# Where the decay masks of the later layers live, and in which order heads and norm blocks are worked off

## What is computed

```python
def step(state, inp):
    xc, lac, bc, cc = inp
    acs = jnp.cumsum(lac, axis=1)
    seg = acs[:, :, None] - acs[:, None, :]
    lmat = jnp.where(mask, jnp.exp(jnp.where(mask, seg, 0.0)), 0.0)
    cb = jnp.einsum('bign,bjgn->bijg', cc, bc)
    y = jnp.einsum('bijgr,bjgrp->bigrp', cb[..., None] * lmat, xc)
    ...
ys = ssd_scan(xs * dtp[..., None], dtp * a, bm, cm)
ys = ys + d_skip * xs
ys = ys.reshape(bsz, s, SSD_INNER) * jax.nn.silu(z)
ysg = ys.reshape(bsz, s, SSD_GROUPS, SSD_INNER // SSD_GROUPS)
ysg = ysg * lax.rsqrt(jnp.mean(ysg * ysg, axis=-1, keepdims=True) + EPS)
ys = ysg.reshape(bsz, s, SSD_INNER) * ssd_norm_w
o_ssd = ys @ ssd_out
```

## Time and profile before

| what | value |
| --- | --- |
| median of 3 runs | 2138.44 us (2137.98 to 2140.2) |
| the profiled execution: its own time | 2139.59 us |
| its span in the profile | 2137.8 us |
| share of the span busy: PE, DVE, ACT, POOL | 99%, 77%, 56%, 3% |
| granted TensorE clock, mean | 0.997 |
| memory traffic over the span | 179 GB/s |

### The profile page before, as it was taken

The page is one execution under the profiler, slowest core; times in us unless marked ns, Lnnn a source line. Parts: engine busy times, 40 slices in busy tenths (PEclk is TensorE's granted clock), DMA queues, the critical chain, the costliest instruction groups (busy, mean ns, idle before and its releaser), DMA issues.

```text
span 2137.8 us, 47790 instructions
## 1 busy us (share of the span) xinstructions
PE 2113.5 (99%) x18652; PEld 2055.5 (96%) x18652; DVE 1640.1 (77%) x2620; ACT 1195.2 (56%) x1803; POOL 58.5 (3%) x54
## 2 busy tenths in 40 slices
PE   9999999999999999999999999999999999999998
PEld 8999999999999999899999999999899999999998
DVE  8987877987877776778957877776678947877764
ACT  6646644565555445546648745445446658845443
POOL 0000000000000000000002200000000002200000
PEclk9999999999999999999999999999999999999999
DMA  7434655654446556554455566556554556565553
GB/s 251 159 128 141 204 190 186 195 171 142 151 157 215 190 189 206 187 168 158 161 190 191 167 203 208 186 187 213 185 169 148 169 183 193 174 201 186 187 189 127
DMA packets 109984, 385.00 MB, mean 180 GB/s; under 512 B 12480, under 2 KB 16768, under 8 KB 109312
## 3 DMA queue, kind: packets, MB, share of 16 engines
q1 hardware_dynamic: 101664, 368.66, 52.2%
q10 hardware_dynamic: 8160, 14.04, 2.1%
HBM read 381.53 MB, written 1.11 MB: 179 GB/s over the span
## 4 chain that ended last, share of the span: by engine, by line
PE 89%; DVE 6%; ACT 2%; issue 2%; DMA 0%; DVEq 0%; ACTq 0%
PE acc L777 25%; PE acc L779 24%; PE acc L778 24%; DVE w_lo L1811 2%; PE acc L896 1%; PE acc L897 1%; PE acc L898 1%; PE acc L841 1%; PE acc L843 1%; PE acc L842 1%; ACT w_hi L1310 1%; PE mid L1133 1%; PE mid L1214 1%; DVE pr L2564 0%; PE mid L964 0%
## 5 line engine op out<-in xcount | busy, mean ns | idle before, releaser
L1811 DVE TENSOR_TENSOR w_lo<-w_raw,w_hi 128x1024 fp32r<-128x1024 f32 x694 | 848.5, 1227 | 306.8 <-ACT w_hi L1310 297.9
L1310 ACT CAST w_hi<-w_raw 128x1024 fp32r<-128x1024 f32 x694 | 724.7, 1047 | 541.3 <-PE acc L779 473.5
L777 PE MATMUL acc<-h_hi,w_hi 128*128 128x256 f32 x2096 | 599.4, 286 | 0.3 <-DVE w_lo L1811 0.3
L779 PE MATMUL acc<-h_hi,w_lo 128*128 128x256 f32 x2096 | 587.5, 280 | 0.0
L778 PE MATMUL acc<-h_lo,w_hi 128*128 128x256 f32 x2096 | 586.3, 280 | 0.0
L777 PE MATMUL acc<-g_hi,w_hi 128*128 128x256 f32 x1456 | 410.0, 282 | 0.8 <-DVE w_lo L1811 0.7
L779 PE MATMUL acc<-g_hi,w_lo 128*128 128x256 f32 x1456 | 407.2, 280 | 0.0
L778 PE MATMUL acc<-g_lo,w_hi 128*128 128x256 f32 x1456 | 406.8, 279 | 0.0
L777 PEld LDWEIGHTS acc<-h_hi,w_hi 128*128 128x128 f32 x2096 | 395.7, 189 | 7.7 <-issue 5.7
L779 PEld LDWEIGHTS acc<-h_hi,w_lo 128*128 128x128 f32 x2096 | 396.1, 189 | 0.0
L778 PEld LDWEIGHTS acc<-h_lo,w_hi 128*128 128x128 f32 x2096 | 395.1, 188 | 0.5
(11 more groups left out here) (434 smaller groups left out, 3394.3 us busy)
## 6 DMA issues: line engine op xcount, KB each, us to landing
w_raw<-weights_d SPq DMA_DIRECT2D x695, 512.0 KB, 3.9
even<-rows_d ACTq DMA_DIRECT2D x16, 256.0 KB, 4.3
odd<-rows_d ACTq DMA_DIRECT2D x32, 128.0 KB, 3.4
p<-p_d ACTq DMA_DIRECT2D x3, 1080.0 KB, 8.5
rdec<-decay_d ACTq DMA_DIRECT2D x2, 768.0 KB, 5.3
p<-p_d SPq DMA_DIRECT2D x1, 1024.0 KB, 10.7
out_d<-work SPq DMA_DIRECT2D x4, 256.0 KB, 2.3
x_all<-x_d SPq DMA_DIRECT2D x1, 516.0 KB, 4.3
```

Source lines behind the costliest of these rows:

```text
L777: mm(dst, wh, hi[:, k, :], start=first and j == 0, stop=False)
L779: done = mm(dst, wl, hi[:, k, :], start=False, stop=last and j == len(ks) - 1)
L1310: nc.scalar.copy(w_hi[:, slot, :], w_raw[:, slot, :]).then_inc(hi_done, 1)
L1811: tt(w_lo[:, slot, :], w_raw[:, slot, :], w_hi[:, slot, :].bitcast(F32), SUB).then_inc(lo_v, 1)
```

## The change

- The product `lseg * cb` is written over the mask itself. `mt`'s space becomes a third mask buffer: `masks` has three, pair b uses `masks[b % 3]`. `pair` on DVE no longer waits for TensorE; `seg` on ACT waits from b = 3 on for `pair_y` b-3 (before: from b = 2 on for `pair` b-2).
- In `ORDER2`, `pair_y` tasks stand two by two (0 and 1 at position 14, 2 and 3 at 18, and so on to 14 and 15 at 37; before, 16 single ones from 17 to 40). The first three `seg` stand at positions 5, 9 and 13 (before: 13, 13, 20), the `cb` tasks at 3, 5, 7, 9 (before: 3, 6, 9, 12).
- The mean's bank is `mid[1]`, and `pair_y` no longer waits for `v_zm`.
- `z_ln` and `z_nt` run three times, over groups (0), (1, 2) and (3), the middle one on two groups at once (`Z_ROOTS`).
- `z_norm`, `z_cast`, `z_low` of blocks 4 to 15 stand at positions 38 to 45, two blocks in each (before: 41 to 47, up to four in one). `z_m` 3 stands at 41 (before: 43).

```diff
 ORDER2 = {
     1: (("rows",),),
     3: (("cb", 0),),
...
-    40: (("pair_y", 15), ("ys", 15), ("z_sq", 12), ("z_mul", 15)),
-    41: (("z_norm", 4), ("z_low", 3), ("z_cast", 4), ("z_norm", 5), ("z_low", 4), ("z_norm", 6), ("z_sq", 13),
...
+    39: (("z_mul", 15), ("z_low", 4), ("z_norm", 6), ("z_cast", 6), ("z_low", 5), ("z_norm", 7), ("z_cast", 7),),
+    40: (("z_low", 6), ("z_norm", 8), ("z_cast", 8), ("z_low", 7), ("z_norm", 9), ("z_cast", 9),),
...
+Z_ROOTS = (0, 1), (1, 3), (3, 4)
...
-        mt = in_arena("mt", 94208, [P, 2, TRI])
+        lseg3 = in_arena("lseg3", 94208, [P, 2, TRI])
+        masks = (lseg[:, 0, :, :], lseg[:, 1, :, :], lseg3[:, :, :])
...
-                if b % 2 and means_ahead(b):
-                    pe.wait_ge(v_zm, at.n * 4 + means_ahead(b))
-                dst = mid[2 + b % 2]
+                dst, mask = mid[2 + b % 2], masks[b % 3]
...
                 pe.wait_ge(p_zsum, at.n * 4 + (g + 1))
-                pe.wait_ge(v_ys, at.n * 16 + values_ahead(g))
-                mm(mid[3][:, 0:T], con1("ones_i"), zq[:, :], start=True, stop=True).then_inc(pe_zm, 1)
+                if g:
+                    pe.wait_ge(v_zm, at.n * 4 + g)
+                mm(mid[1][:, 0:T], con1("ones_i"), zq[:, :], start=True, stop=True).then_inc(pe_zm, 1)
...
-                if b >= 2:
-                    act.wait_ge(v_m, at.n * 16 + (b - 1))
+                if b >= 3:
+                    act.wait_ge(pe_y2, at.n * 16 + (b - 2))
...
-                if b:
-                    dve.wait_ge(pe_y2, at.n * 16 + b)
-                else:
+                if b == 0:
                     dve.wait_ge(v_cb, at.n * 4 + 4)
                 both = cbm[:, b // 4, :].unsqueeze(1).to_broadcast([P, 2, TRI])
-                tt(mt[:, :, :], lseg[:, b % 2, :, :], both, MUL).then_inc(v_m, 1)
+                tt(masks[b % 3], masks[b % 3], both, MUL).then_inc(v_m, 1)
```

More of the change, by code:

```diff
@@ L220 @@
     3: (("cb", 0),),
[L221 to L248, removed]
@@ L257 @@
[L257 to L262, removed]
@@ L263 @@
-    46: (("z_cast", 13), ("z_low", 13), ("z_norm", 15)),
-    47: (("z_cast", 14), ("z_low", 14), ("z_cast", 15), ("z_low", 15)),
+    5: (("cb", 1), ("seg", 0),),
+    7: (("cb", 2),),
+    9: (("cb", 3), ("seg", 1),),
+    13: (("pair", 0), ("pair", 1), ("seg", 2),),
+    14: (("pair_y", 0), ("pair_y", 1),),
+    15: (("ys", 0), ("ys", 1), ("pair", 2), ("seg", 3),),
+    16: (("z_mul", 0), ("z_mul", 1),),
+    17: (("pair", 3), ("seg", 4),),
+    18: (("pair_y", 2), ("pair_y", 3),),
+    19: (("ys", 2), ("ys", 3), ("seg", 5), ("pair", 4),),
@@ new lines @@
+    20: (("z_mul", 2), ("seg", 6), ("pair", 5),),
+    21: (("pair_y", 4), ("pair_y", 5), ("z_mul", 3),),
+    22: (("ys", 4), ("ys", 5), ("seg", 7), ("pair", 6),),
+    23: (("z_mul", 4), ("seg", 8), ("z_mul", 5),),
+    24: (("pair", 7), ("z_m", 0), ("z_ms", 0),),
+    25: (("pair_y", 6), ("pair_y", 7), ("z_ln", 0), ("pair", 8), ("z_nt", 0),),
+    26: (("ys", 6), ("ys", 7), ("seg", 9),),
+    27: (("z_mul", 6), ("pair", 9), ("seg", 10), ("z_mul", 7),),
+    28: (("pair_y", 8), ("pair_y", 9), ("pair", 10),),
@@ new lines @@
+    29: (("ys", 8), ("ys", 9), ("seg", 11),),
+    30: (("z_mul", 8), ("pair", 11), ("seg", 12), ("z_m", 1), ("z_ms", 1), ("z_mul", 9), ("z_norm", 0),
+         ("z_cast", 0), ("z_norm", 1), ("z_cast", 1),),
+    31: (("pair_y", 10), ("pair_y", 11), ("pair", 12), ("z_low", 0), ("z_low", 1),),
+    32: (("ys", 10), ("ys", 11), ("seg", 13), ("z_norm", 2), ("z_cast", 2), ("z_norm", 3), ("z_cast", 3),),
+    33: (("z_mul", 10), ("pair", 13), ("seg", 14), ("z_mul", 11), ("z_low", 2), ("z_low", 3),),
@@ L1685, in pair @@
                     row = upto[b % 2][n]
[L1686 to L1687 removed]
+                    nc.scalar.activation(mask[:, n, 0:T], row, ACT.Relu, scale=-1.0, bias=dts[:, 9, 0, h:h + 1])
+                    last = nc.scalar.activation(mask[:, n, T:TRI], row[:, P:T], ACT.Relu, scale=-1.0,
                                                 bias=dts[:, 9, 1, h:h + 1])
@@ L1690, in pair @@
                 act.wait_ge(a_seg, at.n * 16 + (b + 1))
-                nc.scalar.activation(lseg[:, b % 2, :, :], lseg[:, b % 2, :, :], ACT.Exp, scale=-1.0).then_inc(a_l, 1)
+                nc.scalar.activation(mask, mask, ACT.Exp, scale=-1.0).then_inc(a_l, 1)
                 if b + 2 < NI:
```

46 lines of the change are left out of this document (23 added, 23 removed).

## The result

The changed kernel takes 2148.68 us (median of 5 runs, 2148.23 to 2151.02) where the kernel before takes 2138.44 (5 runs). The ratio is 1.0055, with a 95% interval of 1.0044 to 1.0066: 9 to 14 us slower. All instruction counts of TensorE are the same.

The account below looks back on a forecast made before the run. TensorE, busy 99% of the span, was taken to bound the kernel. Gains of 8.6 us and losses of 14.8 gave net +6.2 on the 2138.44 us median: 2144.6 us, range 2134 to 2151.

Parts of the forecast that it names:

- the turn in the tail: Positions 38 to 45: ACT and DVE wait for each other, 4.35 us a position where TensorE wants 2.82.
- joins: Two `pair_y` in a row on TensorE: the second saves about 0.35 us, 16 times, 5.7 us gained.
- slab 17 in time: First masks made early, one by one, so split 17 isn't late on ACT: 0.8 us gained over two layers.
- POOL's share: Tail, position 40: POOL's work on group 3 slows a `z_low` beside it; taken as 0.8 us.
- the walk: Step-by-step timing of the tail from TensorE's end of slab 37 to low 48: TensorE waits 7.1 us a layer.
- The mean's wait: TensorE waits at mean 3 for POOL's last sum: some 2.5 of the 7.1 us a layer.
- Masks in place: Mask multiply on DVE costs nothing more; new waits 0.3 us a layer, 0.6 us lost, bounds 0 and 1.
- the sum's slow case: Whole forecast with 17 us of tail waits and 2 us of mask waits: +10.4 us.
- The rival that they save nothing: Paired `pair_y`: second pair's loads wait or its mask is late, so no gain; 2150.3 us, chance 0.10.
- Drains at table loads: Rival: four drains at ACT's table loads on the tail's path, 5.5 us more; 2150.1 us, chance 0.03.
- the ring covers the tail: Rival: splits run far enough ahead that tail waits stay under 1 us a layer; 2131.3 us, chance 0.17.
- a part of it: Rival: ACT's splits come sooner, tail turns cost only 3 to 5 us a layer; 2138.4 us, chance 0.20.

Follow-up runs that it names:

- e2: Changed kernel with the second cast of each tail position moved behind the next slab's split; 2140.19 us, 1.0012 of the kernel before.
- e1: Changed kernel with the tail (positions 38 to 47) ordered as before the change; 2133.42 us, 0.9978 of the kernel before.
- e10: e8 with the changed kernel's tail order, two blocks a slab from position 38, last mean at 41; 2152.19 us, 1.0064 of the kernel before.
- e4: Changed kernel with POOL's squares and sums of group 3 cut from 256 columns to 8; 2144.99 us, 1.0039 of the kernel before.
- e5: e2 with masks 3 and 13 multiplied ahead of `z_mul` and the last mean one position later; 2138.28 us, 1.0002 of the kernel before.
- e8: Changed kernel with old tail order, masks 3 and 13 ahead of `z_mul`, and single pairs, odd ones a slab later; 2133.03 us, 0.9982 of before.
- e9: Changed kernel with old tail order and masks of pairs 3, 5, 7, 13 and 15 made or multiplied earlier; 2129.57 us, 0.9961 of before.

## Why the prediction was right, and where it was off

The forecast was 2144.6 us and slower, by gains and losses of unlike size; it came out at 2148.68, inside the range of 2134 to 2151, for the main reason given, the turn in the tail. The sum itself was short: the changed part grew by nearly twice the 6.2 us forecast, as the two largest errors, the tail and the masks, fell on the same side. The stretch, +11.9 us, splits up as follows, from start times:

| term | predicted us | measured us |
|---|---|---|
| joins | -5.7 | -5.0 |
| slab 17 in time | -0.8 | -0.8 |
| the mean's bank | -0.6 | -0.6 |
| old tail's waits gone | -1.5 | -2.3 |
| new waits in the tail | +14.2 | +16.3 |
| waits for second masks | +0.6 | +4.5 |
| sum | +6.2 | +12.1 (stretch 11.9, median 10.2) |

- **The turn** was right as a mechanism and nearly as a size. I had 4.35 us from split to split; the rows are 1214.17 to 1218.53 and 1218.53 to 1222.89 us, 4.36. (The handover of 0.04 us is in none of the rows named for it; after, it is 0.03.) DVE's 1.42 us of idle time ahead of `w_lo`, released by ACT, with the cast right ahead of ACT's split, stand there as described, though not ahead of each `w_lo` of positions 39 to 45 as forecast: ahead of two of them DVE is idle 1.09 us, and ahead of one not at all. e2, e1 and e10 show it by experiment. From E (1197.89, TensorE done with slab 37) low 42 started at 9.6 as walked, low 43 at 16.3 for 15.4, low 44 at 20.6 for 19.8, and low 48 at 37.0 for 36.2. All of the lag is in one step: **POOL's share** of position 40, which I took at 0.8 as a part of the earlier trace rows, is 1.7; e4, where split 43 starts at the 14.6 of the walk without POOL, takes 1.6 of it away. The rows had said 1.09 for one instruction and nothing on the others in the same time; norms beside POOL took 0.71 and 0.83 for 0.48. Further, each stop costs TensorE 0.1 us more at the second product behind it (0.22 for 0.12), six times a layer, which no term held.
- **The mean's wait**: I had 2.5 us of the 7.1 there, and called it a part of the same walk. It was 1.75, since from the start of `z_mul` 15 to the end of POOL's last sum 3.5 us passed (1208.97 to 1212.47) where the old trace had 4.3. With this and with POOL's share slab 44 was late too, where I had 45 to 48. That the wait is a part of the chain e4 and e5 bear out: with it gone, the next slabs start as late as DVE's splits make them.
- **Masks in place** is the mis-sized term, 4.5 us for 0.6, outside its bounds of 0 and 1 and outside the 2 us that the sum's slow case allows. The step that failed is the one that said "nothing" of the multiply and looked only at who frees a buffer. That part holds: no mask waited for its buffer to be read. What I left out is that a join asks for its second mask some 0.7 us behind the first, not a slab later as single pairs do (e8 waits for none), while the table puts one slab or two `z_mul` between that mask and its use. I had worked out the lead of mask 3 at 0.3 us (8.9 against 9.2) and had added that POOL might push DVE over. It did, by 0.8 (the split 0.41 and the multiply 0.41 longer). Pairs 5, 7 and 13 I had not worked out at all, and 0.9 of the 4.5 us came with the slow DMA issue, for which I had no term.
- **Joins**: 0.31 each for 0.355. The rival that they save nothing, by the Trainium skill's rule (TensorE: Matmul & The Clock Gate, Part 3, The mechanism) that a load hides only behind products of another row group, has the row against it: the second pair starts 0.70 us after the first. e8 and e9 bear this out. Yet the changed kernel, at 2148.68, stands nearer to that rival's 2150.3 than to the forecast, and for the rival's other half: "or its mask is late". The chance of 0.10 was too low, as its two causes had the same price and only one was argued against.
- **Drains at table loads** did not come: Ln starts 1.30 us after the load starts, as in the earlier trace rows, where the Trainium skill (ScalarE: Activation LUTs, What ACT_TABLE_LOAD costs) has a further 1.38 us.
- **The other signs.** That the ring covers the tail, or a part of it, is refuted by e1: 16.3 us came back when the old order did. Why the old order has cover is seen by e2: there a norm stands a position ahead of its cast, so ACT can cast and split without waiting.

What stays open is the 1.7 us between the median's +10.2 and the stretch's +11.9. The ratio gives +11.8 on the same runs, so it is within their scatter.

## To carry to other kernels

When two engines hand small pieces to each other inside one step, add up the whole round trip and hold it against the step's length; if it is longer, let each engine take the piece that the other made a step earlier. When two uses are drawn together to save a switch, the second one's input is needed a step sooner: move its making ahead by as much, or the wait eats the gain (5.0 us gained, 4.5 paid, 0.9 of this by chance; all of it kept in e9). A wait that is part of a chain can't be priced where it shows: what counts is how late the chain itself runs. In e5 most of the mean's wait came back at the next slabs; in e4 the chain itself was shortened, and 1.6 us a layer were saved.
